# A transformer step with hierarchical experts on one core: output projection, router and choice of experts by token tile, and experts' rows fetched by indirect transfers

## The chip, the core and the metric

The kernel runs on one core of a Trainium2 chip, in float32. The metric is device time in microseconds of one execution, which takes the weights from DRAM each time. PE is the matrix engine, PEld its weight loads, DVE, ACT and POOL the vector, scalar and GpSimd engines, SP the engine that issues most transfers. Transfers issued by SP run in queue q1, those of POOL in queue q0; both share the core's 16 DMA engines.

## The reference, cut to what matters

One layer for 256 prompt tokens and 64 sampled tokens (N = 320, D = 1024). The part around the change:

```python
x = x + merged @ w_out                               # output projection
h2 = rms_norm(x, norm_ffn).reshape(b * s, D_MODEL)
logit_g = h @ w_rg + b_rg;  grp = argmax(logit_g)    # 4 groups
logit_e = (h @ w_re + b_re)[grp's 8 experts]         # 32 experts in all
top_val, top_idx = top_k(logit_e, 2)                 # 2 experts for each token
y = (silu(xb @ w_gate[e]) * (xb @ w_up[e])) @ w_down[e]   # xb: the rows of expert e
out = zeros.at[slot_tok].add(y * w)                  # back to the tokens
```

Each expert has three matrices of 2 MB (1024x512, 1024x512, 512x1024), so that 201 MB of weights pass through the core in the stage of the experts. There are 640 pairs of token and expert, 20 to an expert on average; a step handles an expert's first 64 rows (SLOTS), and a branch that isn't entered here would handle more.

## The kernel before, in words

The tokens lie in three tiles of 128, 128 and 64 rows (TILES). After attention and the branch products, the kernel goes through the following, in this order on PE.

**Output projection** ("xo", written by `by_token`, matmuls of L612 and, for the tile of 64, of L619). For each tile t and each half c of the 1024 columns, eight products of `mergedT` with w_out (each float32 product is two instructions). DVE adds the PSUM bank to `x` (L1794, L1800, L1803; semaphore x1_done), ACT squares the tile and sums it (`squares`, L1215).

**Transposes and router.** When all six halves are added, PE transposes `x` in 24 pieces (L547, called `transposed("hT2", x)`); DVE and ACT copy them to `hT` and multiply by the norm's gain (L1808, L1389). DVE and ACT write the normalised rows `xn2` (`scaled`). Then PE multiplies by the router's 36 columns in 24 products (L1007) and transposes the per-layer input (`ppT`, L1015).

**Choice of experts** on DVE, for the three tiles at once: logits (L1835), largest group and its index (L1842, L1843), largest two experts in it (L1854, L1855), one-hot `a1`, `a2` and their sum (L1862, semaphore assigned). PE counts every token's rank in its expert in nine products (L1026, "rank"). DVE reads that, builds `rank_a`, and `select` (L1882) makes the one-hot matrix `sel` of expert 0: token by slot. Then come each row's place (L1889 to L1896), the weights and, on POOL, six indirect transfers (L2141) that write the row numbers to `row_of` in DRAM, from where they return as `slot_row` (L2146).

**Stage of the experts.** Slots for nine matrices (EXPERT_SLOTS) hold the weights of three experts. SP issues the gate and up matrices of expert e when `up_done` says that the products of expert e - 3 with them are done, and the down matrix of e when `down_done` says so (`load_next`, `load_down`, L431). All are in one queue in the order gate and up of e + 1, down of e. The matrices of experts 0 to 2 are loaded ahead of the stage; the last two of expert 2 wait for the last output projection (slot 4) and for the router (slot 8, which lies in hT).

The step of expert e on PE (`expert`) is: 16 products with gate and up (`gate_up`, L1060, 32 instructions); `gather` (L1037, 12 instructions), which collects the rows of expert e + 1 as `sel` times `xn2`; the first half of `down` for expert e - 1 (L1084); `turn_rows` (L1045), four transposes of the collected rows; the second half of `down`; `turn_once` (L1074), four transposes of the product of gate and up. ACT copies the collected rows from PSUM to `xg` (L1411), DVE multiplies the transposed rows by the gain (`times_gain`, L1912), which releases the next `gate_up`. ACT applies silu (L1407) and copies the result `ye` (L1418). POOL writes `ye` with an indirect transfer of 128 half rows of 2 KB to `y_rows` (L2151) by `slot_row`. For a slot without a token the index is over `bounds_check`, and its piece isn't moved. The first, plain lines of a step:

```python
gate_up(slots[w_gate], slots[w_up], xe[par], ps[:, 2 + par, :]).then_inc(up_done, 1)
if not last_one:
    gather(sel[1 - par], ps[:, 1 - par, :], sel_ready, e + 2, gathered)
if not first:
    before_down(i, p)
```

Three experts (29 to 31) go back to the tokens by products (`combine`, L593, L598), the others by reading `y_rows` (L2158). The last stage (L577, L568, L612) adds the gated per-layer input and the last norm.

`psum_plan` gives each product of the program its PSUM bank in a rotation and counts releases; `begin`, `finish`, `filled`, `release` and `evacuated` wait and signal by it. `ring_plan` says which product must be done before a slot is loaded again.

## Time and profile before

| | |
|---|---|
| median of 3 runs | 1119.99 us (1116.12 to 1122.78) |
| the profiled execution, its time | 1115.26 us |
| its span | 1113.4 us, mean granted TensorE clock 0.98 |
| busy: PE, PEld | 1063.6 us (96%), 550.4 us (49%) |
| busy: DVE, ACT, POOL | 271.6 us, 233.2 us, 98.9 us |
| bytes moved | 286.32 MB, 257 GB/s over the span |
| output projection | 511.1 to 545.9 us |
| first product of expert 0 | 580.2 us |

The durations come from the profiled execution. Its time is 1.9 us above its span and 4.7 us under the median. Busy time of PE is modelled at its ends, so that a busy PE isn't one at its peak.

### The profile page before, as it was taken

Reading aid. Unit: us, or ns where it says so; the run is one execution under the profiler, and the core shown is the slowest. Engines: PE = TensorE matmul, PEld = TensorE weight load, DVE = VectorE, ACT = ScalarE, POOL = GpSimd, SP = SyncE. Lnnn points to the kernel's source line nnn. Section 1 sums busy time; section 2 is a strip of 40 time slices with the busy share of each in tenths; the row PEclk is TensorE's granted clock in tenths of the full one; section 3 lists DMA queues with packets and bytes.
Section 4 is the critical chain, followed back from the end, with each engine's and each line's share of the span. In section 5 each row is a group of like instructions: output and inputs, shape, how many; then the busy total and the mean of one; then the engine's idle time right before and its main releaser. Section 6 shows DMA issues by size and latency. Waiting matters only on the chain.

```text
span 1113.4 us, 14021 instructions
## 1 busy us (share of the span) xinstructions
PE 1063.6 (96%) x5662; PEld 550.4 (49%) x5662; DVE 271.6 (24%) x729; ACT 233.2 (21%) x488; POOL 98.9 (9%) x142
## 2 busy tenths in 40 slices
PE   6999999999999999999969999999999999999994
PEld 3468877555666667775543333333333333333442
DVE  1122011465433424111241111111111111121413
ACT  2012001166322244000211111111111111111334
POOL 0020031000223220000020000000000000001000
PEclk9999999999999999999969999999999999999997
DMA  9962239220545578563328999999999999999801
GB/s 329 265 214 56 76 75 191 76 76 1 162 130 162 183 283 196 210 227 151 137 90 327 419 422 422 423 424 425 423 422 423 424 424 423 422 421 423 280 1 49
DMA packets 65443, 286.32 MB, mean 257 GB/s; under 512 B 10273, under 2 KB 14650, under 8 KB 44844
## 3 DMA queue, kind: packets, MB, share of 16 engines
q1 hardware_dynamic: 55068, 256.67, 59.8%
q0 software_dynamic: 9936, 28.46, 8.9%
q8 instruction: 41, 0.67, 0.2%
q10 hardware_dynamic: 384, 0.41, 0.1%
q14 instruction: 14, 0.11, 0.0%
HBM read 276.57 MB, written 18.25 MB: 265 GB/s over the span
## 4 chain that ended last, share of the span: by engine, by line
PE 50%; DMA 10%; issue 1%; DVE 1%; ACT 0%; SPq 0%; POOL 0%; POOLq 0%; DVEq 0%
PE ps L1060 17%; DMA ring<-in_w_exp_up_dram 10%; PE ps L556 9%; PE ps L1084 7%; PE ps L1037 6%; PE ps L612 5%; PE ps L1045 1%; PE ps L577 1%; PE ps L1074 1%; PE ps L984 1%; PE ps L619 1%; PE ps L593 1%; PE ps L840 0%; PE ps L547 0%; PE ps L1026 0%
## 5 line engine op out<-in xcount | busy, mean ns | idle before, releaser
L1060 PE MATMUL ps<-ring,reg_xh 128*64 128x512 f32 x512 | 150.4, 602 | 5.0 <-DMA ring<-in_w_exp_up_dram 3.3
L1060 PE MATMUL ps<-late,reg_xh 128*64 128x512 f32 x336 | 148.6, 595 | 2.1 <-DMA reg_k<-in_w_exp_up_dram 1.3
L1037 PE MATMUL ps<-reg_xh 128*64 128x512 f32 x384 | 90.6, 607 | 1.7 <-DVE reg_xh L1882 1.7
L1060 PEld LDWEIGHTS ps<-ring,reg_xh 128*64 128x64 f32 x512 | 47.2, 138 | 89.8 <-issue 88.2
L1407 ACT ACTIVATE reg_xh<-ps 64x512 f32<-64x512 f32 x32 | 34.2, 1068 | 227.8 <-PE ps L1060 227.8
L1946 DVE TENSOR_TENSOR reg_xh<-reg_xh,ps 64x512 f32<-64x512 f32 x32 | 22.1, 691 | 240.5 <-ACT reg_xh L1407 240.5
L1060 PE MATMUL ps<-reg_k,reg_xh 128*64 128x512 f32 x176 | 77.9, 595 | 0.0
L826 PE MATMUL ps<-reg_xh,ring 128*128 128x320 f32 x256 | 73.5, 436 | 0.0
L1060 PEld LDWEIGHTS ps<-late,reg_xh 128*64 128x64 f32 x336 | 44.3, 137 | 46.2 <-issue 44.7
L2151 POOL DMA_INDIRECT y_rows<-reg_xh,slot_row x29 | 28.3, 975 | 395.2 <-ACT reg_xh L1418 354.6
L720 PE MATMUL ps<-reg_xh,ring 128*128 128x285 f32 (+1 forms) x256 | 60.1, 397 | 2.0 <-ACT reg_xh L1258 2.0
L556 PE MATMUL ps<-reg_xh,ring 128*128 128x320 f32 x224 | 60.9, 433 | 0.0
L1037 PEld LDWEIGHTS ps<-reg_xh 128*64 128x64 f32 x384 | 29.2, 140 | 56.2 <-issue 56.2
L826 PEld LDWEIGHTS ps<-reg_xh,ring 128*128 128x128 f32 x256 | 46.8, 190 | 18.2 <-issue 1.6
L720 PEld LDWEIGHTS ps<-reg_xh,ring 128*128 128x128 f32 x256 | 48.6, 190 | 13.3 <-issue 2.2
L556 PEld LDWEIGHTS ps<-reg_xh,ring 128*128 128x128 f32 x224 | 42.3, 190 | 17.6 <-issue 0.4
L1912 DVE TENSOR_TENSOR reg_xh<-ps,gain_e 128x512 f32<-128x512 f32 x32 | 22.1, 691 | 96.3 <-PE ps L1045 96.3
L648 PE MATMUL ps<-ring,reg_xh 128*128 128x512 f32 x96 | 44.4, 620 | 0.9 <-ACT reg_xh L1243 0.9
L1084 PE MATMUL ps<-reg_o,reg_xh 128*64 128x512 f32 x176 | 41.9, 598 | 0.0
L1418 ACT ACTIVATE reg_xh<-ps 128x512 f32<-128x512 f32 x31 | 18.5, 597 | 111.8 <-PE ps L1084 111.8
L1084 PE MATMUL ps<-ring,reg_xh 128*64 128x512 f32 x176 | 41.9, 598 | 0.0
L1084 PE MATMUL ps<-reg_xh 128*64 128x512 f32 x160 | 38.3, 598 | 0.0
(377 smaller groups left out, 1281.9 us busy)
## 6 DMA issues: line engine op xcount, KB each, us to landing
ring<-in_w_exp_gate_dram SPq DMA_DIRECT2D x21, 2048.0 KB, 21.1
ring<-in_w_in_dram SPq DMA_DIRECT2D x13, 2048.0 KB, 11.1
late<-in_w_exp_gate_dram SPq DMA_DIRECT2D x11, 2048.0 KB, 20.1
reg_k<-in_w_exp_up_dram SPq DMA_DIRECT2D x11, 2048.0 KB, 24.6
ring<-in_w_exp_down_dram SPq DMA_DIRECT2D x11, 2048.0 KB, 24.5
ring<-in_w_exp_up_dram SPq DMA_DIRECT2D x11, 2048.0 KB, 25.6
reg_o<-in_w_exp_down_dram SPq DMA_DIRECT2D x11, 2048.0 KB, 25.7
late<-in_w_exp_up_dram SPq DMA_DIRECT2D x10, 2048.0 KB, 25.1
```

The source lines that it names most:

```text
L556: last = pe.matmul(out[:, 0:N], w[:, k, 128 * m:128 * m + 128], moving[:, k, :], start=(k == 0), stop=(k == KT - 1))
L612: last = pe.matmul(out[0:rows, 0:512], stationary[:, k, t0:t0 + rows], w[:, k, cols_], start=(k == 0), stop=(k == n_k - 1))
L648: last = pe.matmul(out[0:rows, :], hT[:, k, s:NP:2] if c == 0 else hT[:, k, 128 * s:128 * s + 128], w[:, k, :], start=(k == 0), stop=(k == ...
L720: last = pe.matmul(out[:, 0:nr * NC], w[:, j, 128 * hid:128 * hid + 128], xt[:, kv, j % 8, r0:r0 + nr, j // 8:j // 8 + NC], start=(j == 0) ...
L826: ins = pe.matmul(ps[:, plan[("gm", m)][0], 0:N], slots[chunk_count(("gm", c))[0]][:, c0:c0 + 128], hT[:, k, :], start=(k == 0), stop=(k = ...
L1037: last = pe.matmul(out[64 * c:64 * c + 64, :], bufs[:, t, :], xn2[:, t, 512 * c:512 * c + 512], start=(t == 0), stop=(t == 2))
L1060: last = pe.matmul(out[64 * part:64 * part + 64, :], xb[:, k, :], ws_[part][:, k, :], start=(k == 0), stop=(k == KT - 1))
L1084: last = pe.matmul(out[64 * c:64 * c + 64, :], hb[:, m, :], w[:, m, 512 * c:512 * c + 512], start=(m == 0), stop=(m == 3))
L1407: act.activation(sg.rearrange("p (m q) -> p q m", m=4), ps[0:64, 2 + par, :].rearrange("p (q m) -> p q m", m=4), ACT.Silu).then_inc(silu_d ...
L1912: return dve.tensor_tensor(out.rearrange("p (c m) n -> p m c n", c=2), ps[:, bank, :].rearrange("p (m c n) -> p m c n", m=4, c=2), gain_e[ ...
L1946: dve.tensor_tensor(sg.rearrange("p (m q) -> p m q", m=4), sg.rearrange("p (m q) -> p m q", m=4), ps[64:128, 2 + par, :].rearrange("p (q m ...
L2151: pool.indirect_dma_start(half_rows, bass.IndirectOffsetOnAxis(ap=target[:, e:e + 1], axis=0), ye[e % 2], None, bounds_check=4 * N - 1, oo ...
```

## The change: what it does

1. PE takes the output projection, the transposes, the router and the ranks tile by tile in a hand-written order: tiles 0 and 2 go ahead, and their transposes, router products and choice of experts lie beside the projection of tile 1. The norm's gain is multiplied into the router's matrix once (`wr`, now 40 columns, 4 of them empty, with a bias of -3e38) instead of into `hT`. `choose` runs once for tiles 0 and 2, once for tile 1.
2. The ranks' products start with those that don't need tile 1; `ppT` stands between them and the last two. The iota of the constants starts at 1, so that `rank_a` is one product instead of two operations. The row places and the weights come after expert 0's rows.
3. Only experts 0 to 3 (SUMMED = 4) get their rows by `gather`. `xn2` is written to DRAM twice (`xn_rows`, four transfers on POOL, 2.6 MB), and POOL fetches the 128 half rows of expert e + 4 into `xg[e % 2]` by an indirect transfer, behind the one that writes `ye` of expert e. From expert 4 on, `turn_rows` waits for the fetch, and `gather`, ACT's copy to `xg` and DVE's `select` fall away.

```diff
-            for t in range(3):
-                for c in range(2):
-                    by_token(("xo", c, t), mergedT, chunk_k(("xo", c)), t)
-            pe.wait_ge(x1_done, 6)
-            transposed("hT2", x)
-            for k in range(KT):
-                evacuated(pe, ("hT2", k))
...
+            mixed_out(0, 0)
+            mixed_out(1, 0)
+            mixed_out(0, 2)
+            turned_half(0, 0)
+            turned_half(0, 1)
+            mixed_out(1, 2)
+            pe.wait_ge(wr_ready, 1)
+            routed(0, 0)
+            routed(0, 1)
+            mixed_out(0, 1, range(4))
+            turned_half(2, 0)
+            turned_half(2, 1)
+            mixed_out(0, 1, range(4, KT))
+            routed(2, 0)
+            routed(2, 1)
+            mixed_out(1, 1, range(4))
+            turned_half(1, 0)
+            mixed_out(1, 1, range(4, KT))
+            routed(1, 0)
+            turned_half(1, 1)
+            routed(1, 1)
+            pe.wait_ge(assigned, 1)
+            out = begin("rank")
...
+            pe.matmul(out[:, 0:32], upper, chosen[:, 0, :], start=True, stop=False)
+            pe.matmul(out[:, 64:96], ones, chosen[:, 0, :], start=False, stop=False)
+            pe.matmul(out[:, 64:96], upper, chosen[:, 2, :], start=False, stop=False)
+            pe.matmul(out[:, 32:64], ones, chosen_02, start=False, stop=False)
+            pe.matmul(out[:, 96:128], ones, chosen_02, start=False, stop=False)
             pe.wait_ge(p_in_s, 32)
...
+            pe.wait_ge(assigned, 2)
+            pe.matmul(out[:, 32:64], upper, chosen[:, 1, :], start=False, stop=False)
+            finish(pe.matmul(out[:, 96:128], ones, chosen[:, 1, :], start=False, stop=True), "rank")
...
-                if not last_one:
+                by_sums = keep in (-1, -2) and p + 1 < SUMMED
+                if by_sums:
                     gather(sel[1 - par], ps[:, 1 - par, :], sel_ready, e + 2, gathered)
...
-                if not last_one:
-                    turn_rows(xg_ready, e + 2, xg_turned)
+                if by_sums:
+                    turn_rows(xg_ready, e + 2, xg[1 - par], xg_turned)
+                elif not last_one:
+                    turn_rows(fetched[1 - par], (i * 3 + (p + 1 - SUMMED) // 2 + 1) * 16, xg[1 - par], xg_turned)
```

DVE's order (`choose(tiles, ts)` holds the operations of the choice of experts, one `max`, `max_index` and so on for each tile):

```diff
+            add_half(0, 0)
+            add_half(0, 1)
+            copy_turned(0, 0)
+            add_half(2, 0)
+            add_half(2, 1)
+            copy_turned(2, 0)
+            rstd(2, 8, 3, slice(0, 3, 2))
...
+            add_half(1, 0)
+            link(choose((0, 2), slice(0, 3, 2)))
+            dve.tensor_tensor(route[:, 920:952], aa[:, 0, :], aa[:, 2, :], ALU.add).then_inc(assigned, 1)
+            add_half(1, 1)
+            copy_turned(1, 1)
+            rstd(2, 9, 4, slice(1, 2))
+            choose((1,), slice(1, 2)).then_inc(assigned, 1)
+            src = filled(dve, "rank")
+            link(dve.tensor_tensor(rank_a.rearrange("p e t -> p t e"), aa, src[:, 0:96].rearrange("p (t e) -> p t e", t=3), ALU.mult))
...
+            select(0, sel[0], 0).then_inc(sel_ready, 1)
+            select(1, sel[1], 0).then_inc(sel_ready, 1)
...
+            times_gain(xe[0]).then_inc(xe_ready, 1)
```

POOL:

```diff
+            pool.wait_ge(xn_dve, 2)
+            pool.wait_ge(xn_act, 1)
+            for k in range(2):
+                pool.dma_start(xn_rows[N * k:N * k + NP, :].rearrange("(t p) n -> p t n", p=128), xn2[:, 0:2, :]).then_inc(xn_out, 16)
+                pool.dma_start(xn_rows[N * k + NP:N * k + N, :], xn2[0:64, 2, :]).then_inc(xn_out, 16)
...
             for e in range(STORED):
                 pool.wait_ge(ye_ready, e + 3)
                 pool.indirect_dma_start(half_rows, bass.IndirectOffsetOnAxis(ap=target[:, e:e + 1], axis=0), ye[e % 2], None,
                                         bounds_check=4 * N - 1, oob_is_err=False).then_inc(ye_out[e % 2], 16)
+                if e == 0:
+                    pool.wait_ge(xn_out, 64)
+                if e + SUMMED < NE:
+                    pool.wait_ge(xg_turned, e + SUMMED - 1)
+                    pool.indirect_dma_start(xg[e % 2], None, xn_half_rows, bass.IndirectOffsetOnAxis(ap=target[:, e + SUMMED:e + SUMMED + 1], axis=0),
+                                            bounds_check=4 * N - 1, oob_is_err=False).then_inc(fetched[e % 2], 16)
```

On SP, slots 3 and 4 are loaded for expert 2 behind `("xo", 0, 1)` and `("xo", 1, 1)`, slot 8 behind `("router", 1)`.

## Rows read from the trace of the kernel before

**Rows 1.** The page's second part: 40 slices of 27.8 us.

```profile
PE   6999999999999999999969999999999999999994
PEclk9999999999999999999969999999999999999997
DMA  9962239220545578563328999999999999999801
GB/s 329 265 214 56 76 75 191 76 76 1 162 130 162 183 283 196 210 227 151 137 90 327 419 422 422 423 424 425 423 422 423 424 424 423 422 421 423 280 1 49
```

**Rows 2.** The chain that ended last, stage of the experts: start us, us, what.

```profile
875.16 7.02 PE ps L1060 x32
882.18 2.58 PE ps L1037 x12
...
889.31 7.04 PE ps L1060 x32
...
896.98 34.93 DMA ring<-in_w_exp_up_dram
...
932.05 7.10 PE ps L1060 x32
...
939.78 37.58 DMA ring<-in_w_exp_up_dram
...
985.04 39.51 DMA ring<-in_w_exp_up_dram
...
1024.69 8.78 PE ps L1060 x32
```

**Rows 3.** Two stretches of that stage: busy us by engine, clock, DMA share, GB/s.

```profile
700.00:800.00 100.00, 100.00 (x482) 34.39 (x480) 14.82 (x29) 15.96 (x22) 6.80 (x7) 1.00 1.01 424
900.00:1000.00 100.00, 96.60 (x467) 36.72 (x465) 17.06 (x40) 14.39 (x20) 6.80 (x7) 1.00 1.01 422
```

**Rows 4.** Timeline from the output projection to expert 0's first products.

```profile
511.13 7.13 PE L612 MATMUL ps<-ring,reg_xh 128*128 128x512 f32 x16 [1.11 <-DVE reg_xh L1788]
...
542.29 3.62 PE L619 MATMUL ps<-late,reg_xh 128*64 128x256 f32 x32
...
546.88 4.65 PE L547 MATMUL ps<-cst,x 128*128 128x128 f32 x24 [0.97 <-DVE x L1803]
...
552.46 7.44 PE L1007 MATMUL ps<-wr,reg_xh 128*128 128x36 f32 x48 [0.92 <-ACT reg_xh L1389]
...
559.83 1.90 PE L1015 MATMUL ps<-cst,reg_pc 128*128 128x128 f32 x6
560.00 0.57 DVE L1835 SCALAR_TENSOR_TENSOR reg_kt<-ps,stat,biasr 128x36 f32<-128x36 f32 x3 [6.07 <-issue]
...
560.81 0.17 DVE L1842 MAX8 reg_kt<-reg_kt 128x8 f32<-128x8 f32 x1
...
567.02 4.05 PE L1026 MATMUL ps<-reg_kt,cst 128*128 128x32 f32 x18 [5.29 <-DVE reg_kt L1862]
...
572.74 5.35 PE L1037 MATMUL ps<-reg_xh 128*64 128x512 f32 x12 [1.67 <-DVE reg_xh L1882]
...
580.23 0.64 PE L1060 MATMUL ps<-late,reg_xh 128*64 128x512 f32 x1 [0.78 <-DVE reg_xh L1912]
```

**Rows 5.** Stretches between projection and experts, columns as in the group of stretches above.

```profile
554.00:571.10 17.10, 11.78 (x60) 10.54 (x59) 6.93 (x45) 2.73 (x6) 0.00 (x0) 0.50 0.55 214
578.00:588.40 10.40, 8.93 (x44) 3.21 (x44) 0.96 (x2) 2.92 (x3) 4.92 (x6) 1.00 0.05 5
```

**Rows 6.** DMA queues from 896 to 1007 us: packets, MB, share of 16 engines.

```profile
DMA packets 5645, 47.02 MB, mean 424 GB/s; under 512 B 795, under 2 KB 795, under 8 KB 953
...
q0 software_dynamic: 600, 0.63, 1.6%
```

**Rows 7.** Transfers from 12 to 38 us, when w_in is read in runs of 2 KB.

```profile
DMA packets 6441, 8.75 MB, mean 337 GB/s; under 512 B 1241, under 2 KB 3322, under 8 KB 6440
```

**Rows 8.** DMA issues, median us to landing.

```profile
y_rows<-reg_xh,slot_row POOLq DMA_INDIRECT x29, 7.2
```

More of the change, by code:

```diff
@@ L994, in _ @@
             pe.wait_ge(normed, KT)
-            for t in range(3):
-                for c in range(2):
-                    by_token(("xo", c, t), mergedT, chunk_k(("xo", c)), t)
-            pe.wait_ge(x1_done, 6)
-            transposed("hT2", x)
-            for k in range(KT):
-                evacuated(pe, ("hT2", k))
-            pe.wait_ge(br_in, 64)
-            out = begin("router")
-            for t, (t0, rows) in enumerate(TILES):
-                for k in range(KT):
-                    last = pe.matmul(out[0:rows, 36 * t:36 * t + 36], hT[:, k, t0:t0 + rows], wr[:, k, :],
-                                     start=(k == 0), stop=(k == KT - 1))
@@ L1009, in _, with mixed_out @@
-            finish(last, "router")
+            def mixed_out(c, t, ks=range(KT)):
+                t0, rows = TILES[t]
+                w = chunk_k(("xo", c))
+                if ks[0] == 0:
+                    begin(("xo", c, t))
+                out = ps[:, plan[("xo", c, t)][0], :]
+                for k in ks:
+                    if t == 2:
+                        last = two_halves(out, mergedT[:, k, t0:t0 + rows], w[:, k, :], k)
+                    else:
+                        last = pe.matmul(out, mergedT[:, k, t0:t0 + rows], w[:, k, :], start=(k == 0), stop=(k == KT - 1))
+                if ks[-1] == KT - 1:
+                    finish(last, ("xo", c, t))
@@ new lines, in turned_half, with routed @@
+            def turned_half(t, half):
+                t0, rows = TILES[t]
+                pe.wait_ge(x1_done, 2 * (0, 2, 1)[t] + half + 1)
+                out = begin(("hT2", t, half))
+                for k in range(4):
+                    c0 = 512 * half + 128 * k
+                    last = pe.transpose(out[:, rows * k:rows * k + rows], x[0:rows, t, c0:c0 + 128], ident[0:rows, 0:rows])
+                finish(last, ("hT2", t, half))
+            def routed(t, half):
+                t0, rows = TILES[t]
+                evacuated(pe, ("hT2", t, half))
+                if half == 0:
+                    begin(("router", t))
+                out = ps[:, plan[("router", t)][0], :]
+                for k in range(4 * half, 4 * half + 4):
+                    last = pe.matmul(out[0:rows, 0:40], hT[:, k, t0:t0 + rows], wr[:, k, :],
+                                     start=(k == 0), stop=(k == KT - 1))
+                if half == 1:
+                    finish(last, ("router", t))
@@ L1016, in _ @@
                 finish(last, ("ppT", k))
-            pe.wait_ge(assigned, 1)
-            out = begin("rank")
-            ones = cst[:, K_UP + 127:K_UP + 128]
-            a_all = route[:, 576:672].rearrange("p (t e) -> p t e", t=3)
-            for t in range(4):
-                for j in range(min(t, 2) + 1):
-                    full_sum = j < t
-                    lhs = ones.broadcast_to([128, 128]) if full_sum else upper
-                    last = pe.matmul(out[:, 32 * t:32 * t + 32], lhs, a_all[:, j, :], start=(j == 0), stop=(j == min(t, 2)))
@@ L1828, in bc @@
                 return ap.unsqueeze(2).broadcast_to([128, 3, n])
-            link(dve.memset(logits, 0.0))
-            link(dve.memset(g8, -3e38))
-            src = filled(dve, "router")
-            dve.wait_ge(br_in, 64)
-            for t, (_, rows) in enumerate(TILES):
-                release(dve.scalar_tensor_tensor(out=logits[0:rows, t, :], in0=src[0:rows, 36 * t:36 * t + 36],
-                                                 scalar=stat[0:rows, 2, 3, t:t + 1], in1=biasr[0:rows, :],
-                                                 op0=ALU.mult, op1=ALU.add), "router")
@@ L1940, in expert_steps @@
                     weigh_slots(keep)
-                if not last_one and keep != 2:
+                if by_sums:
                     dve.wait_ge(gathered, e + 1)
```

296 lines of the change are left out of this document (162 added, 134 removed), and 2 rows, old and new, of the table e.

## The prediction

> **What bounds the kernel now.** I read the slices of the page first [rows 1]. In the last third of the run, slices 22 to 36, two resources look full at once: PE stands at 9 and so does DMA, at 419 to 425 GB/s. A busy PE alone would say that the 2.6 us of products spent per expert on collecting rows are worth taking away. The chain of waits [rows 2] decides between the two. Up to 889 us it is PE in steps: gate and up 7.02 us, collecting 2.58 us, then down and transposes; a step is 889.31 - 875.16 = 14.15 us. Behind that the chain is no longer PE. It is a transfer of an up matrix (34.93, 37.58, 39.51 us from issue to landing), one pass of gate and up, and the next transfer, three experts further on. From 932.05 to 977.5 (939.78 + 37.58 + 0.14) three experts take 45.45 us, so 15.15 us each. The transfers are slower than PE by 1.0 us a step all along; PE only had a lead of three experts, and used it up.
>
> Two stretches agree [rows 3]: the DMA share is 1.01 and the rate 424 GB/s while PE never waits, and 1.01 and 422 when it does. So the stage's end is set by one sum: the moment at which the first refill starts, plus all that the engines then have to move. Three experts are loaded ahead; the first refill waits for the end of expert 0's gate and up (580.23 + 7 = 587.3 us). Between about 567 us and then the DMA engines have nothing to do: slice 20 shows 90 GB/s [rows 1]. What the change can gain is an earlier 587.3. What it can lose is whatever it adds to the queues behind that.
>
> **Part 1: the path to expert 0.** Before, everything small comes behind the projection, which ends at 542.29 + 3.62 = 545.9 us. The first `gather` starts at 572.74, 26.8 us later [rows 4].
>
> Moved ahead of the projection's end are the transposes of tiles 0, 2 and half of 1 (20 of 24: 3.9 of 4.65 us) and the router of tiles 0 and 2 (32 of 48 instructions: 5.0 of 7.44 us, perhaps 4, since most of these rows stood at the lower clock). The projection's own work is the same. I take off 0.8 us for one pause in it that goes, and get 545.9 + 3.9 + 4.2 - 0.8, some 553.3 us; with 0.7 us for pauses of the new order, 554.0. DVE's part for tiles 0 and 2 (18 or so linked operations that take two tiles, 5.3 us by the 0.2 us from one to the next, the MAX8 row being one) lies beside 7 us of projection. `add_half(1, 1)` is queued behind it on DVE and would be late if it grew by over 2 us.
>
> Behind the last projection: DVE's addition 0.9, four transposes 0.9, copy 0.7, eight router instructions 1.0: 557.5 us. Before, the logits began at 560.0 and the ranks at 567.02, so the choice took 7.0 us. For one tile 16 operations of 0.2 us are left, 3.2 us: 560.7 us. PE meanwhile does ten rank instructions (4.05 / 18 = 0.225 each, 2.25 us) and `ppT`, 1.90 us, and is free at 561.7, so now `ppT` is late, not DVE. Four last rank instructions add 0.9 and DVE's product and `select` 0.8 (before: 572.74 - 571.07 = 1.7). The gather starts at 563.4 instead of 572.74: **9.3 us earlier**. From there to gate and up nothing changes (5.35 + 2.1 us), if the clock is the same.
>
> The clock is an unknown of this sum. The trace shows the lower level (0.50, 1.2 GHz) from 554 to 571 us [rows 5], 8 us after dense products ended, and 1.00 from 578.0 on; the gather at 1.2 GHz took 5.35 us, against 2.58 later [rows 2, 4]. In the new order the same small products and DVE's chain still stand for 9 us between the projection and the gather. I take the lower clock as before. Bounds: a clock that stays up gives another 5.35 - 2.58 = 2.8 us and about 1.5 us on the rank and router products; one that is also slow in gate and up costs up to 7 us, though it came back after 5.3 us of dense work before.
>
> The 2.6 MB of `xn_rows` are issued at about 559 us, behind the 2 MB of slot 4 (555 us) and beside the 2 MB of slot 8 (558). At 337 GB/s [rows 7] they need 7.8 us and end by 573, before the first refill at 578. I take nothing; uncovered they would cost up to 7.8 us. The operations moved on DVE behind expert 0's rows and the six `row_of` transfers behind them hold DVE at `slot_rows` for some 3 us. It is needed again 8 us after expert 0's gate and up have ended, so nothing.
>
> **Part 2: what leaves PE.** 28 gathers of 2.58 us, ACT's copies and DVE's selects. PE's step falls from 14.15 to 11.6 us, which only makes it wait 3.8 us for weights where it waited 1.0. **Zero.**
>
> **Part 3: what the queues get.** 28 fetches, none of which the trace before has. The nearest rows are the indirect writes of the same shape: seven in 100 us [rows 3] (POOL's count), 1.6% of the engines for 0.63 MB in 111 us [rows 6]. That is 0.23 us and some 81 KB each, which is 20 rows of 4 KB: dropped pieces cost next to nothing. Lower bound: 28 x 81 KB at 424 GB/s, 5.3 us. By the row of the writes 6.4 us. Reads in runs of 2 KB moved 337 GB/s instead of 424 [rows 7], a quarter more: 8.1 us. Upper bound, if dropped pieces are paid: 262 KB at 424 GB/s is 0.62 us, times 28 is 17.3. I take **7.0 us**, since the writes share the mechanism and differ in direction alone.
>
> Is a fetch ever late? It is issued behind `ye` of expert e, about 12 us into step e + 1, and is needed 9 us into step e + 3: 2 x 11.6 - 3 = 20 us at PE's pace. The writes land after 7.2 us in the same queue [rows 8]; POOL needs 2 us for two. Covered.
>
> **Part 4: the end.** Behind the last up matrix nothing changes. Expert 31's gate and up took 8.78 instead of 7.10 us there, after PE had waited [rows 2]. With a longer wait before it, between 0 and 14.2 - 8.78 = 5.4 us more; I take 0.5.
>
> **Sum.** -9.3 + 0 + 7.0 + 0.5 = -1.8 us. The profiled execution's 1115.3 us become 1113.5. It stands 4.7 us under the median, so that my number for the median is 1120.0 - 1.8 = **1118 us**, no change that shows.
>
> **Rivals.**
> Fetches cost what a full transfer costs (slower). Place: the q0 queue in each of 28 steps. If skipped pieces take their share in reading, or rows scattered over DRAM read badly, a fetch costs 0.62 us: -9.3 + 17.3 + 0.5 = +8.5, 1128.5 us. The sign turns at 0.31 us a fetch, half a per cent is passed at 0.51. Against it stand the writes' 0.23 us, for it that no read was seen. The Trainium skill ("DMA: Bandwidth & Descriptors", section "Measured") holds that transfers under 64 KB are descriptor-dominated and gives 0.95 us of busy time for one of 64 KB; by an estimate from that page the 28 fetches cost some 28 us and the sum would be +19. The writes here don't bear that out beside a full weight queue. 0.17.
>
> The clock stays up over rank and gather (faster). X is then 9.3 + 4.3 = 13.6, and with fetches at 5.3 and nothing at the end -8.3: 1111.7 us. For it speaks that the thin stretch is 9 us instead of 27; against it, that the clock fell after 8. The same sign, smaller, comes from a new order without pauses. 0.28.
>
> PE is the bound after all (faster). Then 28 x 2.58 = 72 us go as well: 1038 us. Against it: DMA at 1.01 throughout, PE waiting from 896 us. 0.03.
>
> PE restarts at 1.2 GHz in every step (slower). With 3.8 us of waiting in each step, gate and up could take 14.2 us, PE's step 18.7, over 15.4: 22 steps x 3.3 = 73 us, 1191. A step without a wait then restarts warm, so it limits itself. The Trainium skill's "TensorE: Matmul & The Clock Gate" (section "HAM oscillation") tells of loops that wait for a DMA in each tile and run cold each time; the trace has one such loss, 1.7 us at 1024.69, but 7.10 us at 932 [rows 2]. 0.03.
>
> Fetches land late, over 20 us: each holds `turn_rows`, 5 us less 3.8 of slack is 34 us in all, 1152. 0.02. That the change doesn't do what it says (rows still by `gather`, or fetches dropped) would leave Part 1 alone, 1110: 0.02.
>
> **How the numbers follow.** A measurement of this kernel can tell about 0.5%, 5.6 us. My forecast has 0.45, with its own range 1113 to 1124: the clock's and the fetch's middle bounds. Faster: 0.28 + 0.03 + 0.02 = 0.33. Slower: 0.17 + 0.03 + 0.02 = 0.22. Same: 0.45. The range reaches from the warm case to the paid fetches, 1110 to 1128.
>
> **What would show it.** The first gather near 563 us and the first refill near 578; DMA share still about 1.01 from there to the last up matrix, three experts per 46.1 us (3 x 0.23 more); q0's share in the stage near 3.3%; PE at 75 to 85% there, waiting for an up matrix from about the tenth expert; the last up matrix landing near 1022. The forecast is wrong if PE still never waits, if the step of the transfers is over 15.7 us, or if the gather starts after 567.

## The result and the profile after

Kernel after: 1122.47 us, median of 20 runs (1118.66 to 1126.27). Kernel before on the same chips: 1119.78 us (20 runs). Ratio 1.0029, 95% interval [1.0016, 1.0042]: the change costs 0.29%, 3.2 us plus or minus 1.5 (the medians differ by 2.7). The forecast was -1.8 us, no change that shows. That class is right, and 1122.47 lies in the range 1110 to 1128. The sign is not right.

The profiled execution took 1122.44 us with a span of 1120.8, 7.4 us more than before (1113.4). Slices of the page of the kernel after, the four lines of [rows 1]:

```profile
PE   6999999999999999999989997877778777797993
PEclk9999999899999999999979999999999999998997
DMA  9962239220545578553379999999999999999601
GB/s 321 259 218 60 75 78 187 75 76 1 156 125 162 173 283 196 221 225 150 125 262 409 420 421 422 420 421 422 423 424 420 421 421 424 421 420 398 216 1 48
```

Slice 21 (counted from 1) moves 262 GB/s where it moved 90: the copy of `xn_rows` now lies in it, and the first refill is issued at 580.5 us instead of 587.35. But slices 37 and 38 still move 398 and 216 GB/s (before 423 and 280), so the transfers end hardly earlier within the span, at about the same slice. In between PE has fallen from 9 to 7 and 8: it waits, as forecast.

Timeline of the kernel after, from the last products of the projection to step 2 of the experts:

```profile
546.52 1.12 PE L1032 MATMUL ps<-wr,reg_xh 128*64 128x40 f32 x16
...
551.55 3.60 PE L1010 MATMUL ps<-late,reg_xh 128*128 128x512 f32 x8
...
564.12 5.04 PE L1087 MATMUL ps<-reg_xh 128*64 128x512 f32 x12 [0.86 <-DVE reg_xh L1963]
...
571.69 0.69 PE L1110 MATMUL ps<-late,reg_xh 128*64 128x512 f32 x1 [1.12 <-DVE reg_xh L1970]
...
585.18 7.09 PE L1110 MATMUL ps<-ring,reg_xh 128*64 128x512 f32 x32 [0.39 <-DVE reg_xh L1970]
...
588.73 1.14 POOL L2242 DMA_DIRECT2D slot_row<-row_of  x2 [6.96 <-DMA row_of<-cst,reg_kt]
...
594.93 0.24 DVE L2016 TENSOR_SCALAR slot_row<-slot_row,cst 128x32 uint32<-128x32 f32 x1 [9.48 <-DMA slot_row<-row_of]
```

The projection began at 514.67 here and at 511.13 before [rows 4]. The diff adds no work ahead of it (only a constant and the place of the router's columns in `wr` differ there), and e8 below, which has the old order, began it at 514.64, all profiled executions of this case between 510.0 and 516.1. So I take these 3.54 us as a difference between two executions. Counted from the projection's start, the gather came after 61.61 us before and comes after 49.45 now, 12.16 us earlier. The last two lines show waits that are new: POOL waits 6.96 us for its own small writes of row numbers, and DVE waits 9.48 us for the row numbers to come back. Before, POOL waited 1.39 us and DVE not at all:

```profile
584.36 1.14 POOL L2146 DMA_DIRECT2D slot_row<-row_of  x2 [1.39 <-DMA row_of<-cst,reg_kt]
...
592.22 0.23 DVE L1923 TENSOR_SCALAR slot_row<-slot_row,cst 128x32 uint32<-128x32 f32 x1
```

The chain that ended last, kernel after, stage of the experts, as in [rows 2]:

```profile
667.53 33.13 DMA ring<-in_w_exp_up_dram
...
700.80 8.80 PE ps L1110 x32
...
710.23 37.33 DMA ring<-in_w_exp_up_dram
...
747.70 7.10 PE ps L1110 x32
...
755.42 38.80 DMA ring<-in_w_exp_up_dram
...
794.36 8.57 PE ps L1110 x32
...
943.50 37.27 DMA ring<-in_w_exp_up_dram
...
980.91 8.80 PE ps L1110 x32
...
990.15 39.60 DMA ring<-in_w_exp_up_dram
...
1029.88 8.56 PE ps L1110 x32
```

The transfers lead from 667 us on instead of 897. From 794.36 to 980.91 twelve experts pass: 15.55 us each, against 15.15 [rows 2]. The step grew by 0.40 us where the forecast had 0.23.

Stretches of the kernel after (columns as in [rows 3]), and its DMA queues from 896 to 1007 us as in [rows 6]:

```profile
554.00:571.10 17.10, 14.12 (x59) 8.26 (x57) 6.30 (x29) 7.82 (x11) 2.50 (x4) 0.70 0.87 326
...
700.00:800.00 100.00, 80.62 (x356) 29.70 (x358) 10.85 (x18) 9.96 (x12) 12.55 (x13) 0.93 1.01 421
...
900.00:1000.00 100.00, 80.60 (x357) 30.22 (x359) 13.87 (x31) 9.97 (x12) 14.26 (x14) 0.93 1.01 422
```

```profile
DMA packets 6105, 46.80 MB, mean 422 GB/s; under 512 B 1160, under 2 KB 1160, under 8 KB 1468
...
q0 software_dynamic: 1120, 1.24, 3.2%
```

PE is busy 80% of the time (forecast 75 to 85), the DMA share is still 1.01, and q0 has doubled, from 600 packets and 1.6% to 1120 and 3.2% (forecast 3.3). So seven fetches take 1.6% of 111 us, 0.25 us each, just the price that the sum used. Yet the step grew by 0.40 us (0.37 by the table of the next section, which takes both kernels over the same experts). That gap is what the experiments are about.

The account of the two profiled executions, with the stage taken from the start of expert 0's gather to expert 31's gate and up:

| piece | before | after | difference |
|---|---|---|---|
| up to the projection's start | 511.13 | 514.67 | +3.5 |
| projection's start to gather | 61.61 | 49.45 | -12.2 |
| gather to gate and up of expert 31 | 451.95 | 465.76 | +13.8 |
| from there to the end of the span | 88.71 | 90.92 | +2.2 |
| span | 1113.4 | 1120.8 | +7.4 |

### The profile page after: what moved, and what is told of

Same layout as the page of the kernel before. It is cut to its first block, busy times and chain, and to the rows that moved or that the text cites. A ratio compares the mean times of both kernels' runs of the same rounds, so it can differ in the third digit from the quotient of the medians.

```text
span 1120.8 us, 13356 instructions
## 1 busy us (share of the span) xinstructions
PE 1011.9 (90%) x5322; PEld 535.2 (48%) x5322; DVE 264.7 (24%) x710; ACT 215.7 (19%) x460; POOL 131.1 (12%) x174
## 4 chain that ended last, share of the span: by engine, by line
PE 34%; DMA 27%; issue 1%; DVE 1%; ACT 0%; SPq 0%; POOL 0%; DVEq 0%; POOLq 0%
DMA ring<-in_w_exp_up_dram 27%; PE ps L1110 11%; PE ps L560 8%; PE ps L1134 3%; PE ps L1010 3%; PE ps L616 2%; PE ps L1087 1%; PE ps L581 1%; PE ps L988 1%; PE ps L623 1%; PE ps L597 1%; PE ps L1032 0%; PE ps L1095 0%; PE ps L844 0%; SPq L435 0%
## 5 line engine op out<-in xcount | busy, mean ns | idle before, releaser
L1110 PE MATMUL ps<-ring,reg_xh 128*64 128x512 f32 x512 | 165.0, 650 | 46.5 <-DMA ring<-in_w_exp_up_dram 27.9
L1110 PE MATMUL ps<-late,reg_xh 128*64 128x512 f32 x336 | 162.0, 639 | 24.0 <-DMA reg_k<-in_w_exp_up_dram 22.9
L1110 PEld LDWEIGHTS ps<-ring,reg_xh 128*64 128x64 f32 x512 | 52.3, 149 | 141.2 <-issue 125.5
L1110 PE MATMUL ps<-reg_k,reg_xh 128*64 128x512 f32 x176 | 84.7, 638 | 0.0
L1110 PEld LDWEIGHTS ps<-late,reg_xh 128*64 128x64 f32 x336 | 47.2, 146 | 70.3 <-issue 68.8
L1134 PE MATMUL ps<-ring,reg_xh 128*64 128x512 f32 x176 | 42.0, 598 | 0.0
L2187 POOL DMA_DIRECT2D late<-in_cache_kv_dram x32 | 19.3, 602 | 189.9 <-issue 189.9
L1134 PE MATMUL ps<-reg_xh 128*64 128x512 f32 x160 | 38.5, 599 | 0.0
L560 PE MATMUL ps<-late,ring 128*128 128x320 f32 x128 | 34.7, 433 | 0.0
L560 PE MATMUL ps<-reg_o,ring 128*128 128x320 f32 x128 | 34.6, 432 | 0.0
## 6 DMA issues: line engine op xcount, KB each, us to landing
ring<-in_w_in_dram SPq DMA_DIRECT2D x13, 2048.0 KB, 10.8
```

The costliest lines, as they stand in the source:

```text
L560: last = pe.matmul(out[:, 0:N], w[:, k, 128 * m:128 * m + 128], moving[:, k, :], start=(k == 0), stop=(k == KT - 1))
L1110: last = pe.matmul(out[64 * part:64 * part + 64, :], xb[:, k, :], ws_[part][:, k, :], start=(k == 0), stop=(k == KT - 1))
L1134: last = pe.matmul(out[64 * c:64 * c + 64, :], hb[:, m, :], w[:, m, 512 * c:512 * c + 512], start=(m == 0), stop=(m == 3))
L2187: pool.dma_start(slc_in[b % 2][64 * half:64 * half + 64, :, cols_].rearrange("p l (a d) -> p l a d", d=DH), page_rows(b, half)[:, :, 8 + 4 ...
```

## The experiments

The theory, which the experiments then test: the 16 DMA engines don't carry the indirect transfers evenly. A transfer names 128 half rows, of which some 40 are real; the slots from 0 to about 19 hold them, so the same partitions are filled for every expert. The weights are split evenly (before, the sixteen increments of the up matrices of experts 1 and 4, ahead of most of the pieces, lie within 0.8 and 0.4 us), so the engines that also carry the pieces fall further behind with each expert, and a weight matrix has landed only when the slowest has its part. The profile's share is a mean over 16 engines and can't show that. The trace has another record: the sixteen increments of a load's semaphore. From the first to the last of them, in us, for the gate matrices of experts 7, 10, ... 31, the nine in the same slots (worked out from the trace; the last column is the mean time per expert between the landings for experts 13 and 28):

```
kernel                      first ... last of the nine loads                us/expert
before                      1.8  3.6  4.3  5.0  5.8  6.7  7.6  8.3  9.0     15.18
after                       3.7  6.0  8.2  9.8 11.2 12.9 14.3 15.8 17.5     15.55
e1_order_alone              1.8  4.0  4.4  5.6  6.3  7.2  8.0  8.7  9.5     15.17
e2_fetch_dropped            2.1  3.0  5.5  6.2  7.0  7.9  8.7  9.4 10.5     15.24
e3_fetch_twice              4.2  7.4 11.4 13.6 15.7 18.3 20.6 23.1 24.7     15.93
e4_fetch_shifted            2.4  2.7  3.3  3.1  3.0  3.3  2.7  3.1  3.8     15.35
e5_order_shifted            1.7  3.0  3.3  3.1  3.1  3.1  3.0  2.8  2.8     15.07
e6_fetch_crowded            2.4  6.1 10.7 14.0 17.5 20.6 24.3 24.6 24.8     16.02
e8_fetch_alone              2.7  5.0  7.9  9.5 10.9 12.6 14.1 15.5 17.1     15.55
e9_order_rotated            1.8  2.8  3.1  2.8  2.7  2.7  2.8  2.7  3.1     15.07
e11_order_ahead             1.5  3.5  4.3  5.2  5.8  6.9  7.6  8.3  9.2     15.17
```

Already in the kernel before the spread grows by 0.3 us an expert, by its writes alone; with the fetches it grows by 0.6.

A second table takes the stage (from the first gather to the start of expert 31's gate and up, in the profiled execution, against 451.95 us before) beside the timed ratios:

| kernel | stage, us | ratio to before, interval |
|---|---|---|
| after | +13.8 | 1.0029 [1.0016, 1.0042] |
| e1_order_alone | +3.1 | 0.9914 [0.9890, 0.9939] |
| e8_fetch_alone | +11.9 | 1.0116 [1.0088, 1.0143] |
| e2_fetch_dropped | +5.5 | 0.9948 [0.9930, 0.9967] |
| e7_dropped_no_copy | +6.6 | 0.9947 [0.9926, 0.9968] |
| e3_fetch_twice | +24.6 | 1.0136 [1.0115, 1.0158] |
| e4_fetch_shifted | +7.2 | 0.9978 [0.9963, 0.9992] |
| e6_fetch_crowded | +32.2 | 1.0189 [1.0149, 1.0229] |
| e5_order_shifted | -1.4 | 0.9868 [0.9843, 0.9893] |
| e9_order_rotated | -0.4 | 0.9905 [0.9887, 0.9922] |
| e11_order_ahead | -0.4 | 0.9902 [0.9886, 0.9918] |
| e10_rotated_ahead | -2.5 | 0.9874 [0.9857, 0.9891] |

The runs were made in three groups (e1 to e4, e5 to e8, e9 to e11); before had medians of 1118.06, 1118.9 and 1116.39 us in them. The ratio of after has a group of its own.

### The two halves of the change, each alone

**e1_order_alone** has the new order and still gathers for all experts; **e8_fetch_alone** is the kernel before with the fetches.

```diff
-                by_sums = keep in (-1, -2) and p + 1 < SUMMED
+                by_sums = not last_one
...
-                elif not last_one:
-                    turn_rows(fetched[1 - par], (i * 3 + (p + 1 - SUMMED) // 2 + 1) * 16, xg[1 - par], xg_turned)
```

> The new order of projection, router and choice alone; rows of all experts by gather, no copy of the normalised rows, no fetch. All theories that call the transfers the bound: the gain at the start (10.2 us, counted from the start of the projection to the first refill) stays, the 11.9 us that the stage grew go: about 1110 us, ratio to before 0.991. The step of the transfers is back at 15.15 us. Rival (PE still shares the bound): slower than the kernel with fetches, over 1122, since 28 gathers of 2.58 us come back.

> The kernel before with the fetches alone, in its old order. The transfers are the bound, so the 28 gathers that go give nothing and the fetches cost 0.42 us each: 1.010 to 1.012 of before, 1130 to 1132 us. Rival (PE shares the bound): faster than before.

Measured: e1 1107.75 us, -0.86%; e8 1133.29 us, +1.16%. Their sum, +0.30%, is what both together do (+0.29%): the two halves add up, and the change is a gain of 9.6 us and a loss of 13 us. e1 lies 2 us under the 1110 expected, and e8 1.3 us over its range, with the ratio inside. The chain of e1, stage of the experts:

```profile
888.35 35.73 DMA ring<-in_w_exp_up_dram
...
931.94 37.56 DMA ring<-in_w_exp_up_dram
...
977.18 39.36 DMA ring<-in_w_exp_up_dram
```

Without the fetches three experts take 45.4 us (931.94 + 37.56 - 888.35 - 35.73), and PE leads until 888, as before until 897. With them the step is 15.55 in e8 as in after. Between e1 and after the stage grows by 10.7 us, 0.38 a fetch; between before and e8 by 11.9, 0.43.

### What of a fetch costs: its pieces, its number

**e2_fetch_dropped** issues all fetches with a bound that drops every half row but the first, so that experts 4 to 31 compute on stale rows. **e7_dropped_no_copy** does the same and writes only 64 rows of `xn_rows` instead of the 2.6 MB. **e3_fetch_twice** issues each fetch a second time, into a buffer that nobody reads.

```diff
-                                            bounds_check=4 * N - 1, oob_is_err=False).then_inc(fetched[e % 2], 16)
+                                            bounds_check=0, oob_is_err=False).then_inc(fetched[e % 2], 16)
```

```diff
+                    pool.indirect_dma_start(reg_x[:, 0:512], None, xn_half_rows, bass.IndirectOffsetOnAxis(ap=target[:, e + SUMMED:e + SUMMED + 1], axis=0),
+                                            bounds_check=4 * N - 1, oob_is_err=False).then_inc(fetched_other, 16)
```

> The changed kernel with all 28 fetches issued, but the bound set to 0, so that all pieces but those of the first half row are dropped; the rows of experts 4 to 31 are then not the tokens' (left out of the computation). Theory A (the 16 DMA engines carry a fetch unevenly, the fullest sets the step) and theory B (the bytes read cost more than those written, evenly): a dropped piece costs little, 28 x 0.03 to 0.1 us, so 1111 to 1114 us, step of the transfers 15.2. Theory C (a fixed price for each indirect transfer, whatever it moves): 1121 to 1123 us, as with fetches, step 15.55.

> Fetches issued with the bound at 0 as before (rows of experts 4 to 31 left out), and of the copy of the normalised rows only 64 rows are written, 0.26 instead of 2.6 MB. If the copy is hidden in the gap before the first refill, as was forecast: as with the full copy, ratio 0.995. If it costs something: down to the order alone plus the dropped pieces, 0.992 to 0.993.

> The changed kernel with each fetch followed by a second one of the same rows into a region that is free then; the result is the same. All theories that charge the fetch to the DMA queues: another 28 x 0.42 = 11.5 us, 1134 us, step of the transfers 15.96. If the 11.9 us of the stage came from elsewhere (the lower clock of gate and up after waits, DVE's late slot_rows at the start): under 1128.

Measured: e2 1112.69, e7 1113.64, e3 1133.91 us. The empty fetches put the ratio 0.34% over e1's, with intervals that overlap; the stage shows 2.4 us more in e2 and 3.5 in e7, 0.08 and 0.12 a fetch. e7 is not faster than e2: the copy of `xn_rows` costs nothing that shows, as the prediction said. The second fetch adds 10.8 us to the stage (24.6 - 13.8), 0.38 each, as much as the first: from one fetch to two the cost is linear. Chain of e3:

```profile
856.87 38.21 DMA ring<-in_w_exp_up_dram
...
904.64 38.24 DMA ring<-in_w_exp_up_dram
...
952.45 38.19 DMA ring<-in_w_exp_up_dram
```

952.45 - 904.64 = 47.8 us for three experts, 15.94 each: another 0.39 on 15.55. The spread grows by 0.8 us an expert. All three met their expectations.

### Where the rows lie

Up to here the theory could still be only a dear fetch. **e4_fetch_shifted** and **e6_fetch_crowded** move the same bytes with the same transfers and change only the slots, by a few more operations on DVE ahead of the stage: in e4 the rows of each expert from the fourth on start 20 slots further on than those of the expert before (modulo the number of slots); in e6 the first 20 rows lie in slots 0 to 9 and 32 to 41. Both compute the whole reference.

```diff
+    c[:, K_SHIFT + 4:K_SHIFT + STORED] = 20 * np.arange(STORED - 4) % SLOTS
...
+                link(dve.tensor_tensor(i1, i1, rk, ALU.add))
+                pk = place[:, 3 * k:3 * k + 3]
+                link(dve.tensor_scalar(pk, i1, float(SLOTS), -float(SLOTS), ALU.is_ge, ALU.mult))
+                link(dve.tensor_tensor(i1, i1, pk, ALU.add))
```

> The changed kernel, computing the same, but the rows of experts 4 to 28 lie in their 64 slots rotated by 20 slots more for each expert, so that their rows aren't always in the lowest slots. Bytes, pieces and transfers are the same for writes and fetches. Theory A (uneven load of the 16 engines, since about 20 rows in the lowest slots go to the same engines each time): both kinds of transfer come to their mean price, 0.24 instead of 0.3 to 0.4 us, the step falls from 15.55 to about 15.35, 5 to 7 us in all: 1116 to 1118. Theory B (even, but a higher price of reading) and C: no change, 1121 to 1123, step 15.55.

> The changed kernel, computing the same, but an expert's first 20 rows are put in slots 0 to 9 and 32 to 41 instead of 0 to 19, for experts 4 to 28. Theory A with the pieces dealt to the engines in pairs of neighbouring slots, pair i to engine i modulo 16: five engines now have twice the load, 0.64 instead of 0.32 us in each of the two transfers, so the step grows by some 0.6 us and the time by 14 to 16: 1136 to 1139 us. Theory A with eight neighbouring slots to an engine: the fullest engine has eight pieces either way, no change, 1122. Even load: no change.

Measured: e4 1115.40 us, just under its 1116 to 1118 and 0.51% under after (0.9978 against 1.0029, intervals apart); e6 1141.79 us, 1.60% over it. In e4 the spread stays at 3 us from the second load to the last; in e6 it reaches 24 us and the step 16.0. Of e6's time not all is the placement's: its longer chain on DVE sends the `row_of` writes later into the first refill, and 4.9 of the 18.4 us by which its stage exceeds that of after are lost before the gate matrix of expert 7 has landed (89.2 us after the gather began, 84.3 in after). So it came out over the 1136 to 1139 us expected, while its step grew by 0.47 us and not by 0.6. The steps, taken from expert 13 to 28, are free of the start. Chain of e6, and its queues in the window of [rows 6]:

```profile
863.15 38.47 DMA ring<-in_w_exp_up_dram
...
911.18 38.56 DMA ring<-in_w_exp_up_dram
...
959.30 38.07 DMA ring<-in_w_exp_up_dram
```

```profile
q0 software_dynamic: 1120, 1.25, 3.2%
```

That is the line of after but for the last digit of its MB, and e4 has 1120 packets, 1.24 MB and 3.2% as well. With one and the same mean load three placements give steps of 15.35, 15.55 and 16.02 us. That is the theory's point: what counts is the busiest part, and the share doesn't show it. The bytes, the pieces and the rows in DRAM are the same; only the partitions differ.

How much it should be can be estimated. 0.25 us of 16 engines is 4.0 us of engine time. If 10 of them carry it, each has 0.40, close to the step's growth. The Trainium skill ("DMA: Bandwidth & Descriptors", section "The descriptor swizzle") gives groups of four neighbouring partitions to an engine in a plain POOL transfer of 1 MiB to 128 partitions; by an estimate from that page 20 filled slots in both halves load 10 of 16 engines, in keeping with 0.40. I had assumed pairs of slots, which gives 10 as well. Both rules put twice the pieces of after on the busiest engines in e6, so the runs don't tell them apart, and the records name no engine. The third rule of the expectations, eight neighbouring slots to an engine, asked for no change in e6 and is excluded. Which partition goes to which engine stays open, and so does whether it is the engines themselves that are loaded unevenly or a path to the partitions behind them: the increments would look the same. Nor is all of the price the last part's. From expert 13 to 28 the first of the sixteen increments also comes later with each expert, every 15.04 us in after against 14.91 before, 0.13 of the 0.37.

**e5_order_shifted** is e1 with slots turned as in e4, to see what the writes alone lose by the same cause. Its turned slots are used in writing only, so that experts 4 on add their rows to other tokens; the work is the same. **e9_order_rotated** (below) does it for the whole computation.

> The new order alone, with gather for all experts, and the rotation of the slots by 20 for each expert, which now touches the writes of the results alone. Theory A (uneven engines): the writes too cost their mean price, 0.2 instead of 0.32 us, so the step falls from 15.16 to about 15.03 and the time by some 3.5 us below the order alone: ratio to before 0.988, 1105 us. Rival: the writes' unevenness is absorbed, since the engines run ahead of one another: no change, ratio 0.991.

Measured: 1105.27 us, ratio 0.9868; spread 3 us, step 15.07. The stage is 4.5 us shorter than in e1, and that of e10 (below) 2.1 shorter than that of e11, where the turning is again the only difference in the stage: the kernel before loses some 2 to 4 us by its own writes. e4 minus e9 (both turned, with and without fetches) is now the price of an evenly dealt fetch: 7.5 us of stage, 0.27 each, and 0.73% (0.9978 against 0.9905), 8.2 us. That is close to the 0.25 of the forecast. From e1 to after, with the slots not turned, it was 10.7.

### What the new order loses at the start

The stage of e1 is 3.1 us longer than before, with the same transfers. In the timeline the six `row_of` writes now fall beside the first refill. e1:

```profile
588.46 1.14 POOL L2235 DMA_DIRECT2D slot_row<-row_of  x2 [8.85 <-DMA row_of<-cst,reg_kt]
...
594.87 0.24 DVE L2014 TENSOR_SCALAR slot_row<-slot_row,cst 128x32 uint32<-128x32 f32 x1 [13.50 <-DMA slot_row<-row_of]
```

POOL waits 8.85 us for the last of them and DVE 13.50 for what it reads; behind DVE's wait the product of expert 1's gate and up and the gains of expert 2 are queued, and PE waits 1.2 us in turn. A stretch of e1 at the first refill:

```profile
580.00:584.00 4.00, 3.61 (x21) 1.45 (x21) 1.02 (x2) 0.00 (x0) 0.00 (x0) 1.00 0.86 250
```

In after itself the loss looks different. Its gate and up of expert 0 ran in part at the lower clock (granted 0.57 from 572 to 576 us), so that the first refill was issued 16.4 us after the gather began (14.6 before, 14.8 in e1) and 6.1 us after the first of the small writes (4.2 in e1). The first 14 us from the first refill on, before, after and e1:

```profile
587.40:601.40 14.00, 12.91 (x64) 4.54 (x62) 2.81 (x6) 2.69 (x3) 0.00 (x0) 1.00 0.83 312
```

```profile
580.50:594.50 14.00, 12.92 (x64) 4.65 (x62) 1.71 (x3) 2.73 (x3) 2.10 (x4) 1.00 0.87 310
```

```profile
576.40:590.40 14.00, 12.91 (x64) 4.54 (x62) 1.71 (x3) 2.75 (x3) 3.74 (x5) 1.00 0.82 227
```

After moves 310 GB/s as before (312), e1 227. And DVE's hold of 9.5 us delays no load in after: the down matrix of expert 3 is issued 18.7 us behind the first refill, as before, and 21.0 us in e1. The loss has nearly the same size all the same: counted from the gather's start, the gate matrix of expert 7 landed after 80.1 us before and 83.0 in e1, and with the fetches after 81.6 in e8 and 84.3 in after, 2.9 and 2.7 us more.

The experiments e9, e10 and e11 test what the small writes do. **e11_order_ahead** moves the row places ahead of `times_gain` of expert 0, where DVE is idle; **e9** turns the slots in the choice matrix and in the places; **e10_rotated_ahead** has both.

```diff
-            dve.wait_ge(gain_e_in, 16)
-            dve.wait_ge(xg_turned, 1)
-            times_gain(xe[0]).then_inc(xe_ready, 1)
...
             dve.tensor_copy(placei, place).then_inc(ranked, 1)
+            dve.wait_ge(gain_e_in, 16)
+            dve.wait_ge(xg_turned, 1)
+            times_gain(xe[0]).then_inc(xe_ready, 1)
```

> The order of the change, gather for all experts, and each expert from the fourth on keeps its rows in slots turned by 20 per expert, in the choice matrix as well as in the placement, so that the whole reference is computed. Theory (the 16 DMA engines carry the row writes unevenly, and the slowest sets the step): as e5_order_shifted, 1105 us, ratio to the kernel before 0.985 to 0.990, step of the transfers 15.05 to 15.12 us an expert, spread of an up load's sixteen increments about 3 us at the end instead of 9.5. Rival (the gain of e5 over e1 came from elsewhere, or the two further operations on the rows' places delay the start): ratio 0.991 or more, as e1_order_alone, with the first refill some 3 us later.

> e9_order_rotated with the rows' places worked out before the gains of expert 0 instead of behind them, so that the six writes of row numbers leave before the first refill of the weights. Theory (in the joined order these writes and the reads that follow share the queues with the first refill and slow it by some 3 us): 1102 us, ratio 0.982 to 0.987, 3 us under e9, about 4.2 MB moved in the first 14 us from the refill on instead of 3.0, VectorE without its wait for slot_row. Rival (the refill's slow start is owed to something else, or is made up later): within 1 us of e9.

> e1_order_alone with the rows' places worked out ahead of the gains of expert 0, as in e10_rotated_ahead. Theory: 3 us under e1_order_alone, 1105 us, ratio 0.986 to 0.991, step 15.16 us and spread near 9 as in e1. Rival (the writes do not slow the refill): as e1_order_alone, 1107.75 us, ratio 0.991 to 0.993.

Measured: e9 1105.07, e10 1101.38, e11 1104.69 us. e11's timeline, and the same stretch:

```profile
575.38 1.14 POOL L2235 DMA_DIRECT2D slot_row<-row_of  x2 [1.39 <-DMA row_of<-cst,reg_kt]
```

```profile
580.00:584.00 4.00, 3.42 (x20) 1.65 (x22) 1.43 (x4) 0.13 (x1) 0.00 (x0) 1.00 1.01 428
```

POOL's wait is back to 1.39 us, DVE's is gone, and from 580 to 584 us 428 GB/s are moved instead of 250. The stage is 3.5 us shorter than e1's. The DMA rates over 52 us show the second place of the loss, first e9, then e10 (from 573 us, slices of 1.3 us; the first refill is issued at 573.4 and 574.1):

```profile
GB/s 0 189 271 372 435 410 404 416 416 303 151 340 429 415 429 416 447 422 441 429 457 389 147 183 365 435 416 416 429 435 416 470 429 441 416 366 422 435 416 416
```

```profile
GB/s 0 88 233 416 422 416 435 410 421 366 95 189 422 416 435 435 429 416 429 435 451 416 397 410 435 422 391 416 447 422 470 435 429 416 353 422 422 422 429 416
```

A dip at slices 10 to 12 is in both. The hole at slices 23 and 24 (147 and 183 GB/s, 602 to 604 us) is in e9 alone: gate and up of expert 2, held by DVE, frees its slots late. In e10 it isn't there, though the waits are not gone as they are in e11: POOL still waits 4.3 us and DVE 6.7, where the longer chain for the turned slots sends the last small write at 573.6 us, just ahead of the refill. The stage gives 2.1 us, the medians 3.7 (0.9905 against 0.9874; the intervals just touch). The theory had 3 us for both, so the stage bears out two thirds of it in e10 and all of it in e11; e11's timed ratio doesn't stand clear of e1's, which is from another group.

Not every number met its expectation. The 3.0 MB in the first 14 us from the refill on, expected of e9 too, are seen in e1 (3.1), e7 (2.9) and e6 (2.5), not in e9 (4.3) or after (4.3); e9 lost its time at the second hole. And e9's ratio (0.9905) is short of the 0.985 to 0.990 expected, while its time and its spread are those of e5.

e10 computes the whole reference and is faster than both kernels: 1.26% under before, 1.55% under after.

## Why the prediction was right and wrong

**What bounds the kernel**: right. Taking the products of 28 gathers off PE gained nothing; PE's share fell to 80% and the DMA share stayed at 1.01.

**Part 1**: direction right, size off. The gather came 12.2 us earlier and not 9.3. The excess lies beside the projection: its last products ended 40.5 us after its start (551.55 + 3.60 - 514.67), where the forecast had 42.9. Two terms were mis-sized. The 20 transposes were put at 3.9 us, five sixths of the 4.65 before, and took 2.4 (1.10 + 0.71 + 0.60). The router of tiles 0 and 2, put at 4.2 us from rows of which most stood at the lower clock, took 3.1 (1.98 + 1.12):

```profile
532.20 1.10 PE L1021 MATMUL ps<-cst,x 128*128 128x128 f32 x8
...
536.83 1.98 PE L1032 MATMUL ps<-wr,reg_xh 128*128 128x40 f32 x16
...
542.25 0.71 PE L1021 MATMUL ps<-cst,x 64*128 64x64 f32 x8
```

From the last router products on the forecast had 5.9 us to the gather, and it took 5.6. The clock: the stretch from 554 to 571.1 ran at a mean of 0.70 and not 0.50, and the gather took 5.04 instead of 5.35, so the low clock was taken rightly. It also lay over gate and up of expert 0 in the profiled execution: from the gather's start to the end of that pass 16.35 us instead of 14.57. The prediction had named that as a bound, up to 7 us, and put it at nothing. This is 1.8 us of after's late start. Without it the loss would not have been smaller by as much: e2's profile has the lower clock there and e7's has not (16.27 against 14.38), and yet e2's stage is the shorter by 1.1 us. e7's earlier refill met the `row_of` writes (210 GB/s in its first 14 us) and its loads were held, by 2.4 us from the down matrix of expert 3 on, as in e1.

**The hidden work**: the copy of `xn_rows` cost nothing (e7). The step "hold DVE at `slot_rows` for some 3 us ... so nothing" failed: DVE was held 9.5 us, since the small writes had come beside the refill. In after's profile this delayed no load (above); in e1, with an earlier refill, it did, and the order of e11 undoes it and saves 3.5 us of stage. What e11's order would give after itself was not run. The prediction had named the cover (8 us after gate and up of expert 0) but its 3 us suit the trace before, in which the queues were empty and POOL waited 1.39 us.

**Part 3, the step that failed most.** "I take 7.0 us": right as a mean, wrong as what the step pays. Fetches cost 0.25 us of the engines' mean (q0's share) and 0.38 to 0.43 of the stage, 10.7 to 11.9 us. The price lies inside the bounds (5.3 to 17.3) and past the 0.31 that the prediction gave as the point where the sign turns. The error was one of reading: the share in [rows 6] is over 16 engines, and the row was taken for the load of each. The trace before could have told, by the increments' spread of 9.0 us at the last load. The cause named in the rival (skipped pieces paid in full, 0.62 us) wasn't it: a fetch with nearly all of its pieces dropped cost 0.08 to 0.12 us (e2, e7). The figure of 0.95 us for a transfer of 64 KB from the Trainium skill ("DMA: Bandwidth & Descriptors", section "Measured") is a span of one transfer by itself. It fits neither 0.25 nor 0.43: for what a transfer adds to a full weight queue the measurement decides.

**Part 4**: gate and up of expert 31 took 8.56 us, against 8.78 before: 0.2 less instead of 0.5 more. But the end of the program grew by 2.2 us, which no step had: all of it lies behind the last output, in POOL's closing DRAIN (last section).

**The sum** by measured terms, against before: -12.2 (order, to the gather) + 3.1 (the late start of the refills, from e1) + 10.7 (28 fetches, e1 to after) + 2.2 (end) = +3.8, and 3.5 that lie ahead of the projection make the 7.4 of the spans, but for rounding. The timed difference is 2.7 by the medians and 3.2 plus or minus 1.5 by the ratio; the profiled execution of before was 4.5 us under its median, that of after at its median. From the forecast's -1.8 to +3.8 it is -2.9 (order), +3.1 (start, put at nothing), +3.7 (fetches) and +1.7 (end). With 7.0 for the fetches and the rest as measured the sum is +0.1, so that the fetch is the largest error but not the only one, and the gather's excess made up for 2.9 us of them.

**The rivals.** PE cold in every step did not come: gate and up often took 8.8 us after a wait (clock 0.93), but only 1.7 us more each time, and inside the slack. The Trainium skill's loop that runs cold behind each DMA wait ("TensorE: Matmul & The Clock Gate", section "HAM oscillation") is present here in that mild form and costs nothing, as 15.55 us a step is the transfers' own. No fetch was late: PE never waited for one in after.

## What to carry to other kernels

A DMA share in a profile is a mean over 16 engines, but a load is done when the last of its sixteen parts is: for small transfers that always fill the same few partitions, reckon with the busiest part (here 0.40 us by the estimate, 0.38 to 0.43 measured, instead of 0.25), and look at the spread of a load's sixteen increments, which here grew from load to load where the parts were unequal. Turning the place of the rows from one transfer to the next costs a few operations once and took back 0.5% (e4 against after). When work is moved ahead, look at what the small transfers behind it now collide with: POOL's wait for the same six writes was 1.4 us on empty queues and 8.9 beside the weights (e1).

## What the runs showed that was not expected

- The placement of the same 40 half rows changes an expert's step from 15.35 to 16.02 us at one and the same DMA share (e4, after, e6). The spread stops growing at some 25 us in e6, and grows more slowly near there in e3.
- An indirect transfer with nearly all of its pieces dropped still costs 0.08 us of a full queue (e2 against e1; 0.12 in e7).
- Every kernel with fetches (after, e2, e3, e4, e6, e7, e8) ends 90.9 to 93.0 us after the start of expert 31's gate and up, every one without 87.1 to 88.7. In after the last issue of an output is at 1109.59 us, 11.2 us ahead of the span's end; in before it was 8.8. The data have landed 2.8 us after the issue in both. So 28 fetches add 2.4 us, whatever they move, and the second 28 another 1.1. What the drain waits for, no run here shows. The rest of the differences at the end is the length of expert 31's gate and up (7.1 to 9.8 us).
- Where PE waits, its granted clock falls to the lower level now and then: 0.93 over 100 us, a pass of gate and up of 8.8 us instead of 7.1. Behind a bound set by DMA it cost nothing.
